# V's second half in three rounded passes, its split made on chip by ScalarE and VectorE

## What is computed

```python
def peer_ffn(h, w_q, sub_k1, sub_k2, u_tab, v_tab):
    ...
    idx = jnp.take_along_axis(cand_i, pos, axis=-1)      # 8 heads x 16 experts of 16384 per token
    g = jax.nn.softmax(top_s, axis=-1).astype(h.dtype)

    def chunk(args):
        xc, ic, gc = args
        u = jnp.take(u_tab, ic, axis=0)
        act = jax.nn.gelu(jnp.einsum('chkd,cd->chk', u, xc), approximate=False)
        return jnp.einsum('chk,chkd->cd', gc * act, jnp.take(v_tab, ic, axis=0))
```

## Time and profile before

| | |
|---|---|
| runs | 2657.42, 2661.69, 2661.08 us; median 2661.08 |
| profiled execution | 2662.42 us, span of its instructions 2660.6 us |
| mean granted TensorE clock | 0.969 |
| PE busy | 2502.0 us (94%) |
| DVE busy | 1559.0 us (59%) |
| POOL busy | 890.6 us (33%) |
| ACT busy | 507.0 us (19%) |

### The profile page before, as it was taken

One profiled execution on the slowest core, in us unless ns is written; L12 is line 12 of the kernel. 1 busy time (PEld: TensorE's weight loads), 2 busy tenths in 40 slices (PEclk: granted clock), 3 DMA queues, 4 the chain that ended last, 5 costly groups with the idle time before them and its releaser, 6 DMA issues.

```text
span 2660.6 us, 30288 instructions
## 1 busy us (share of the span) xinstructions
PE 2502.0 (94%) x11270; PEld 1776.3 (67%) x11270; DVE 1559.0 (59%) x3250; ACT 507.0 (19%) x1060; POOL 890.6 (33%) x650
## 2 busy tenths in 40 slices
PE   5988899999999999999978788999999999999995
PEld 4756699889444566666656567988964446666663
DVE  1345479967455554655445447896755555456654
ACT  2344432133000000000043344212310000000001
POOL 3400360000444544555353215200024445355551
PEclk8999999999999999999989798999999999999997
DMA  6455334654999998999835612365479999899992
GB/s 257 136 190 190 121 111 137 190 147 139 377 388 394 381 383 304 367 389 379 309 122 153 182 41 82 105 191 167 141 271 385 389 382 387 302 376 382 389 374 106
DMA packets 219889, 679.46 MB, mean 255 GB/s; under 512 B 32385, under 2 KB 63153, under 8 KB 219233
## 3 DMA queue, kind: packets, MB, share of 16 engines
q1 hardware_dynamic: 142912, 396.42, 43.8%
q0 software_dynamic: 76832, 281.11, 27.7%
HBM read 658.87 MB, written 18.56 MB: 255 GB/s over the span
## 4 chain that ended last, share of the span: by engine, by line
PE 89%; DVE 3%; DMA 3%; ACT 3%; issue 1%; SPq 1%; POOL 1%; ACTq 0%; DVEq 0%
PE ps L943 33%; PE ps L954 32%; PE ps L657 4%; PE ps L658 4%; PE ps L659 4%; PE ps L932 2%; PE ps L839 2%; PE ps L820 2%; DMA arena<-gelu_half 1%; PE ps L688 1%; PE ps L680 1%; PE ps L829 1%; PE ps L907 1%; DMA arena<-in_w_mod 1%; DMA ring<-in_w_mod 1%
## 5 line engine op out<-in xcount | busy, mean ns | idle before, releaser
L943 PE MATMUL ps<-arena,ring 128*128 128x256 f32 x4096 | 916.7, 380 | 0.0
L954 PE MATMUL ps<-ring,arena 128*128 128x512 f32 x2048 | 901.4, 592 | 1.4 <-DVE arena L1803 1.3
L943 PEld LDWEIGHTS ps<-arena,ring 128*128 128x128 f32 x4096 | 774.2, 190 | 156.7 <-issue 60.3
L954 PEld LDWEIGHTS ps<-ring,arena 128*128 128x128 f32 x2048 | 388.5, 190 | 441.1 <-issue 434.5
L576 POOL DMA_INDIRECT arena<-in_u_rows,arena x256 | 296.4, 1158 | 867.8 <-PE ps L932 534.0
L1803 DVE SCALAR_TENSOR_TENSOR arena<-arena 128x256 f32<-128x256 f32 x256 | 108.7, 425 | 570.4 <-ACT arena L1169 367.2
L576 POOL DMA_INDIRECT arena<-in_v,arena x256 | 335.3, 1310 | 311.7 <-DVE arena L1826 202.2
L1169 ACT ACTIVATE arena<-ps 128x256 f32<-128x256 f32 x256 | 98.3, 384 | 1601.5 <-PE ps L943 1432.1
L536 POOL TENSOR_TENSOR ring_lo<-ring,ring_hi 128x1024 fp32r<-128x1024 f32 x84 | 216.8, 2592 | 427.3 <-ACT ring_hi L1054 427.3
L1826 DVE SCALAR_TENSOR_TENSOR arena<-arena 128x1024 f32<-128x1024 f32 x254 | 325.6, 1282 | 23.3 <-DMA arena<-in_v,arena 5.8
L1812 DVE CUSTOM_DVE_ANT_0 arena<-arena 128x1024 f32<-128x1024 f32 x256 | 305.5, 1221 | 13.5 <-DMA arena<-in_u_rows,arena 13.3
(11 more groups left out here) (213 smaller groups left out, 2133.8 us busy)
## 6 DMA issues: line engine op xcount, KB each, us to landing
ring<-in_u SPq DMA_DIRECT2D x256, 512.0 KB
ring<-in_v SPq DMA_DIRECT2D x256, 512.0 KB
ring<-in_w_mod SPq DMA_DIRECT2D x80, 512.0 KB
ring<-in_w_in SPq DMA_DIRECT2D x36, 512.0 KB
ring<-in_w_q SPq DMA_DIRECT2D x32, 512.0 KB
gelu_half<-arena SPq DMA_DIRECT2D x120, 128.0 KB, 3.8
arena<-gelu_half SPq DMA_DIRECT2D x120, 128.0 KB
arena<-in_w_mod SPq DMA_DIRECT2D x16, 512.0 KB, 18.6
```

Source lines behind the costliest of these rows:

```text
L943: ins = mm(ps[:, 6 + b % 2, 0:STOK], slot[c % RING][:, P * k:P * k + P], HFS[:, k, :], start=(k == 0), stop=(k == KC - 1))
L954: ins = mm(ps[:, t + 3 * q, :], GL[:, b % GLS, P * t - P:P * t], slot[c % RING][:, 512 * q:512 * q + 512], start=(b == MIDDLE[0]), stop=(b ...
```

## The change

For blocks 64 to 127 the outer products are made from split operands. The hidden products stay as they are, and so do the first 64 outers.

- ACT gets two more copies in each block: `high_w(b)`, the rounded half of the gated activations (256 columns), and `high_v(b)`, the rounded half of V's block (1024 columns).
- DVE gets two subtractions: `low_w(b)` (256) and `low_v(b)` (1024), the remainders. low_v is what now frees V's ring slot.
- PE's outer(b) becomes 12 rounded matmuls with 512 columns moving in place of 4 plain ones. It waits for `ws_lo` (low_w's signal) and for low_v.
- The halves lie in room that the gates of blocks 0 to 63 leave: two halves for each of four blocks of activations (`w_split`) and three of V (`v_split`). `vs_spent` tells that an outer is done.
- The dots of a block are divided, one ahead of low_w and two behind low_v.

```diff
+Q_WS = Q_WORK + D
+Q_VS = Q_WS + 2 * GLS * STOK
+VSLOTS = 3
...
                 def outer(b):
 
                     c = v_chunk(l, b)
+                    if b >= SPILL:
+                        pe.wait_ge(used(c % RING), turn_of(c))
+                        pe.wait_ge(sem("ws_lo"), since("ws_lo", l) + b - SPILL + 1)
+                        for t in range(1, NT):
+                            r = slice(P * t - P, P * t)
+                            for q in range(2):
+                                n = slice(512 * q, 512 * q + 512)
+                                for i, j in ((0, 0), (0, 1), (1, 0)):
+                                    ins = mm(ps[:, t + 3 * q, :], w_half(b, i)[:, r], v_half(b, j)[:, n], start=False,
+                                             stop=(b == KEYS - 1 and i == 1), skip_group_check=True)
+                        ins.then_inc(sem("vs_spent"), 1)
+                        return
...
+                def high_v(b):
+
+                    if b < SPILL + VSLOTS:
+                        products_done(min((Q_VS - Q_G + 2 * D * (b - SPILL + 1) - 1) // STOK, MIDDLE[-1]))
+                    else:
+                        act.wait_ge(sem("vs_spent"), since("vs_spent", l) + b - SPILL - VSLOTS + 1)
+                    wait_loaded(act, v_chunk(l, b))
+                    fn(v_half(b, 0), slot[v_chunk(l, b) % RING], ACT.Copy).then_inc(sem("vs_hi"), 1)
+
+                def high_w(b):
+
+                    act.wait_ge(sem("w_ready"), since("w_ready", l) + b + 1)
+                    fn(w_half(b, 0), GL[:, b % GLS, :], ACT.Copy).then_inc(sem("ws_hi"), 1)
+
                 for b in range(SPILL, KEYS):
                     if b == SPILL:
                         gelu(b)
+                    high_w(b)
+                    if b == SPILL:
+                        high_v(b)
                     if b + 1 < KEYS:
                         gelu(b + 1)
+                    if b + 1 < KEYS:
+                        high_v(b + 1)
...
+                def low_v(b):
+
+                    c = v_chunk(l, b)
+                    dve.wait_ge(sem("vs_hi"), since("vs_hi", l) + b - SPILL + 1)
+                    tt(v_half(b, 1), slot[c % RING], f32(v_half(b, 0)), ALU.subtract).then_inc(used(c % RING), 1)
+
+                def low_w(b):
+
+                    dve.wait_ge(sem("ws_hi"), since("ws_hi", l) + b - SPILL + 1)
+                    tt(w_half(b, 1), GL[:, b % GLS, :], f32(w_half(b, 0)), ALU.subtract).then_inc(sem("ws_lo"), 1)
+
...
                 for b in range(SPILL, KEYS):
                     product(b)
+                    if b == SPILL:
+                        low_v(b)
+                    if dots < P - 3:
+                        dot(dots)
+                        dots += 1
+                    low_w(b)
+                    if b + 1 < KEYS:
+                        low_v(b + 1)
                     if b == SPILL + QUARTER:
                         diagonals(2 * l + 1)
-                    for _ in range(3):
+                    for _ in range(2 if b < SPILL + 14 else 3):
                         if dots < P:
                             dot(dots)
                             dots += 1
```

More of the change, by code:

```diff
@@ L129 @@
 Q_LN, Q_GT, Q_DIAG, Q_WORK = Q_G, Q_G + 2 * D, Q_G + 4 * D, Q_G + 5 * D
+Q_WS = Q_WORK + D
+Q_VS = Q_WS + 2 * GLS * STOK
+VSLOTS = 3
+assert Q_VS + VSLOTS * 2 * D <= Q_G + SPILL * STOK
 SIGNALS = {
@@ L144 @@
     **dict.fromkeys(("gelu", "w_ready"), [128, 128]),
+    **dict.fromkeys(("vs_hi", "vs_spent", "ws_hi", "ws_lo"), [KEYS - SPILL, KEYS - SPILL]),
     **dict.fromkeys(("row_used",), [256, 256]),
@@ L192, in build @@
                       enumerate(("x_hi", "x_lo")))
+        ws, vs = in_slab("w_split", Q_WS, 2 * GLS * STOK), in_slab("v_split", Q_VS, VSLOTS * 2 * D)
         const = sb("const", C_N)
@@ L226, in build, with w_half, v_half @@
         HFP = ar(Q_HFP, KC * P).rearrange("p (k t) -> p k t", k=KC)
+        def w_half(b, i):
+            at = 2 * STOK * (b % GLS) + STOK * i
+            return ws[:, at:at + STOK]
+        def v_half(b, i):
+            at = 2 * D * ((b - SPILL) % VSLOTS) + D * i
+            return vs[:, at:at + D]
         def modulated(n, k, kn, t):
@@ L1166, in gelu @@
                     if b >= SPILL:
-                        c = start["uv", l] + 2 * SPILL - GLS + b - SPILL if b < SPILL + GLS else v_chunk(l, b - GLS)
-                        act.wait_ge(used(c % RING), turn_of(c))
+                        if b < SPILL + GLS:
+                            c = start["uv", l] + 2 * SPILL - GLS + b - SPILL
+                            act.wait_ge(used(c % RING), turn_of(c))
+                        else:
+                            act.wait_ge(sem("vs_spent"), since("vs_spent", l) + b - GLS - SPILL + 1)
                     fn(GL[:, b % GLS, :], ps[:, 6 + b % 2, 0:STOK], ACT.Gelu).then_inc(sem("gelu"), 1)
@@ L1198, in experts, with products_done @@
                             part(p)
+                def products_done(e):
+                    act.wait_ge(sem("w_ready"), since("w_ready", l) + MIDDLE.index(e) + 1)
+                def high_v(b):
+                    if b < SPILL + VSLOTS:
+                        products_done(min((Q_VS - Q_G + 2 * D * (b - SPILL + 1) - 1) // STOK, MIDDLE[-1]))
+                    else:
+                        act.wait_ge(sem("vs_spent"), since("vs_spent", l) + b - SPILL - VSLOTS + 1)
[4 more added lines that the diff above has]
+                    fn(w_half(b, 0), GL[:, b % GLS, :], ACT.Copy).then_inc(sem("ws_hi"), 1)
                 for b in range(SPILL, KEYS):
@@ L1465, in residual @@
                         if t:
-                            c = v_chunk(n // 2, KEYS - 1)
-                            dve.wait_ge(used(c % RING), turn_of(c))
+                            dve.wait_ge(sem("vs_spent"), since("vs_spent", n // 2 + 1))
                     else:
```

## The result

| | before | after |
|---|---|---|
| median | 2661.28 us | 2781.91 us (2767.07 to 2789.32, 4 runs) |
| ratio | | 1.045, 95% interval 1.0403 to 1.0497 |
| profiled execution | 2662.42 us | 2777.68 us, span 2775.8 |
| PE busy | 94% | 89% |
| DVE busy | 59% | 63% |

The change costs 120.6 us where I had forecast 27, and the time lies above the range. The kernel after also spreads more: 22 us between its fastest and slowest run, 4 us before.

The account below looks back on a forecast made before the run. PE alone was taken to set the second half's pace, 6.88 us a block; afterwards a DVE-ACT ring of 7.24. Terms gave +11.7 a layer, +13.4 with one clock fall, two layers +27: 2688 us, range 2625 to 2745.

Parts of the forecast that it names:

- loads come no later: SP's loads of U and V: low_v frees V's slot well before the old outer's end; costed at nothing.
- one fall a layer: PE's waits of 2 to 3.5 us at blocks 64, 83, 97 drop its clock to half: 1.7 us a layer.
- rival 2: Clock falls in PE's gaps, adding 1.7 us to a block's 6.17: 26 us a layer, 2740 us; chance 0.15.
- The ring: DVE and ACT waiting on each other in turn, blocks with three accumulates: 7.24 us a block, longer than PE's 6.17.
- The sum without V: Block-by-block sum for one layer, late V costed at nothing: +11.7 us, with one clock fall +13.4, two layers +27.
- dots: 14 second-half blocks with dots: 6.70 us each by DMA's rate, for 6.88 before, -2.5 us a layer.
- over to accumulates: Where accumulates begin: the hidden-to-outer path first shows, with the weights' multiply ahead of it, +1.1 us.
- block 96: Its two diagonals on DVE, 1.22 us each, hidden before, now in the DVE-ACT ring: +2.4 us.
- the path: From hidden(b)'s end to outer(b), through ACT and DVE: 8.06 us, 7.12 a block; with dots 7.00, 6.59 a block.
- rival 3: DVE's subtraction low_v runs at 2.66 us as L1435 does: 60 us a layer, 2809 us; chance 0.04.
- Rival 1: DMA decides accumulate blocks at 391 GB/s, 6.58 us each, the DVE-ACT ring being shorter: 2625 us; chance 0.10.
- rival 4: The split is covered and PE decides throughout, high_v running ahead of high_w and gelu: 2573 us; chance 0.05.

Follow-up runs that it names:

- no_gather: The changed kernel without 250 of the 256 row gathers of a layer, dots and accumulates working on six rows; 2671.23 us (one run).
- v_first: The changed kernel with SP loading V(b) ahead of U(b+1) in the second half; 2680.07 us, ratio 1.008.
- act_order: v_first with ACT making high_v(b+1) ahead of high_w(b) and gelu(b+1), DVE's order kept; 2591.45 us, ratio 0.9743.
- ready: The changed kernel with only block 64 split, outers of blocks 65 to 127 reading its halves in twelve rounded passes; 2574.44 us (one run).
- plain_outer: v_first with second-half outers as four plain float32 matmuls on the rounded halves, split work and waits kept; 2726.39 us, ratio 1.0246.
- reorder: act_order with DVE also taking low_v(b+1) ahead of low_w(b) and the first dot; 2595.43 us, ratio 0.976.
- diag_early: act_order with the two gate diagonals of the layer's end made at block 79 and not in block 96; 2587.31 us, ratio 0.9727.
- v_late: v_first with SP holding V(b) back until hidden(b-1) is done, still ahead of U(b+1); 2688.89 us, ratio 1.0106.
- v_ahead: reorder with the load of V(b+1) called one place sooner, ahead of U(b+1); 2605.58 us, ratio 0.9799.

## Why the prediction was wrong

**The step that failed** is "loads come no later ... with the rows that is less than the bytes now moved ... I cost these at nothing". I looked at when V is called and at how many bytes move, not at how long one chunk takes to land. It lands 6.23 us after its call in the median before the change (first layer, 1030 to 1330 us), and up to 7.5; that was hidden, since outer(b) wanted it only 10.3 us after the call (the end of outer(b-2) to the start of outer(b), a hidden, an outer and a hidden). high_v wants V a full hidden and outer earlier than outer(b) did. The lead shrank to 7.2 us (the median in no_gather, where nothing holds ACT up; 7.27 in the block shown), just when the call also came to stand behind U's. There V took 7.05 us in the median and over 10 in the slowest tenth. I had written the price of a late V, "high_v and all behind it move by as much", and gave it no chance and no rival. ACT's waits for V come to 81.3 us. On PE the idle time before the outers is 65 us longer than in v_first, and the added time at half clock costs at most 34 more; with that, 99 at most, the 94.7 us that v_first gives back are accounted for.

**The clock.** I counted one fall a layer, there were 9 and 7. The count without late V was about right (v_first 1 and 2, no_gather 1 and 0). The cause that rival 2 named, the ring's steady idle time (1.07 us a block by my sum, 0.8 in the trace), is refuted by v_first: behind some 85 gaps of 0.7 to 1.8 us stands one fall. The Trainium skill (TensorE: Matmul & The Clock Gate, A second HAM failure mode: psum-queue depth-cycling) describes a clock that swings because PE idles briefly and often between groups of matmuls. The trace of v_first, with these 85 gaps, does not show that; the falls of the kernel after stand behind fewer and longer gaps, 2.2 us and more in layer 0.

**The ring** was right: 7.24 us a block forecast, 7.23 to 7.24 measured in v_first, in no_gather and in the blocks of the kernel after that no late V touches. v_first's accumulates moved 352 GB/s (355 forecast). It also answers to its cure: 6.38 expected for act_order, 6.35 measured.

**The sum without V.** Mine was +11.7 a layer and +27 in all with one fall in each. v_first, which has three falls, is 22.6 us over the kernel before beside it, so the sum was some 4 us too high. By terms, in layer 0 of v_first: dots 6.1 to 7.2 by turns, 6.66 in the mean (6.70); between, 6.19 (6.17); over to accumulates, 8.16 (7.24 + 1.1 = 8.34); accumulates 7.23 or 7.24 (7.24); block 96, 9.50 (9.64). The block with two accumulates and the one behind it are 6.1 to 6.2 and 8.2 to 8.35, 7.2 in the mean (7.12). The 6.70 for dots was right by luck: I took it from DMA's rate, yet in ready the same blocks take 6.19 with the same rows, and in v_first no dot waits for its row. Blocks by turns long and short, and 7.00 with the plain outers of plain_outer, fit the path instead, which I had summed to 6.59 and set aside.

**low_v** was 1226 ns, priced at 1.22; rival 3 is refuted. The passes are 0.226 apart at full clock, as priced.

**DMA's ceiling.** I took 391 GB/s as the most it moves; act_order and reorder moved 402 over 270 us. Rival 1's price was too high by that, and rival 4, which I held for impossible by ACT's list, is what a changed list comes close to (2587 for diag_early against 2573).

**What stays open.** Why a chunk takes 6 to 7 us to land at less than full rate was not taken apart; by no_gather the rows' traffic is 2.7 of V's 7.05 us. Why some gathered rows come late in diag_early, and why some long gaps bring no fall, was not followed up.

## What to carry to other kernels

A new first reader of a buffer moves the load's due time, even if the slot is freed sooner: take the time from the call to the new due time, and compare it with the landing that the trace shows under that traffic, not with bytes over bandwidth. Two engines that hand work to and fro in each iteration form a ring whose length is the sum of both parts, whatever their busy shares; take out of it what waits for neither (here the copy of V), but move the loads first, or the cure is worse than the ring. And a wait on TensorE's side can bring a stretch at half clock behind it, as most of those of 2.2 us and more did here: it is then dearer than its own length.

## What the runs showed of the hardware

- Two 512 KB loads called 0.38 us apart under gathers do not land together: in v_late the first after 7.16 us, the second after 9.19 (medians). Without the gathers 4.34 was seen for the second of the pair.
- Gaps of 0.7 to 1.8 us on PE, some 85 of them in v_first, brought one fall of the clock (behind a gap of 1.8). In layer 0 of the kernel after there were twelve gaps of 2.2 us and more; nine stood at a fall, and three, of 3.83, 2.49 and 2.38 us (before blocks 102, 71 and 121), had none. The length of a gap alone does not decide.
- DMA moved 400 to 405 GB/s over 270 us in ready, reorder, act_order and v_ahead, with an estimated 59% of the bytes in gathered rows (2.91 x 0.524 of 2.57 MB a block); the middle before the change, the best stretch of the earlier trace rows, had 391.
